# Building a routing table by adding single weights in DRAM in place of one-hot matmuls

## The chip, the cores and the metric

The kernel runs on one core of one Trainium2 chip. The metric is the device time of one execution in microseconds, the median of three runs.

## What is computed

The reference is two blocks, one behind the other, on 512 tokens of width 1024 in float32: first a two-layer block of modulated feed-forwards, a pooling mixer and a convolution mixer, then a block with stick-breaking attention, a recurrent branch and a retrieval layer over 16384 single-neuron experts. Only the retrieval layer (and the low parts of weights in it) is touched:

```python
q = jnp.einsum('td,dhk->thk', xc, w_query)                       # 8 heads, two halves of 128
s = jnp.einsum('thpk,hpnk->thpn', q, sub_keys)
top_s, top_i = lax.top_k(s, 16)                                  # 16 of 128 keys, per half
cand_s = top_s[:, :, 0, :, None] + top_s[:, :, 1, None, :]       # 256 pairs
best_s, best_pos = lax.top_k(cand_s, 16)
idx = take(cand_i, best_pos)                                     # cand_i = i0 * 128 + i1
g = jax.nn.softmax(best_s, axis=-1)
u, v = expert_u[idx], expert_v[idx]
act = jax.nn.gelu(jnp.einsum('td,thkd->thk', xc, u))
return jnp.einsum('thk,thkd->td', g * act, v)
```

So each token has 8 heads x 16 experts = 128 weights g, and a pair of heads may name the same expert, in which case their weights add.

## The kernel before

The kernel doesn't gather experts. It computes the activations of all 16384 experts for all 512 tokens, multiplies them by a dense table of weights (zero where a token hasn't chosen an expert), and multiplies the result by all of expert_v. Experts are numbered 128 n + m; a column m is the 128 experts with that m, n on the partitions, tokens along the free axis.

**The stream of weights.** All weight matrices come as 599 groups of 128 x 1024 float32 (512 KB) from DRAM. For each group c, SyncE loads `raw`, ScalarE rounds it to `whi` (line 499, helper `hi`), another engine forms the low part `wlo = raw - whi` (line 445, helper `lo`, on GpSimd throughout), and TensorE runs 24 matmuls of 512 columns (`three`, lines 1450 to 1452: high by high, high by low, low by high). There are four buffers of each, and `hi` of group c + 3 is issued beside group c.

**The up stage** is 128 groups, a column each: TensorE writes a bank, ScalarE applies the gelu (line 790) and stores 256 KB to the DRAM tensor `expert_acts` (line 783). **The down stage** is 128 groups too: for each column m a 256 KB piece of weights (`g_ring`, line 843) and of activations (`act_in`, line 844) is read back, VectorE multiplies them (`we32`, line 1426), ScalarE rounds, VectorE takes the rest (line 1430), and TensorE multiplies eight such columns at a time by eight groups of expert_v.

**The table.** In the up stage's first 32 columns (the lead: 8 columns for each 128 tokens) VectorE runs `best_pairs(tt)`: the top 16 of 256 pairs per head, the two expert numbers (`chosen[0]`, `chosen[1]`), the softmax (ScalarE's exponential, line 815, stands behind the eight columns in its queue). TensorE waits for `chosen_ready`, transposes the three rows (line 1765), and VectorE copies them to `pick` (`take_turned`), the weight split in three bf16 parts. In the columns 32 to 127, four sections of 16 columns with a chunk of 8 tokens each (64 chunks) and 8 without, `rows` on VectorE makes one-hot matrices (`hot_m`, `hot_n`, and `hot_w` by parts 0 and 1, lines 1405 to 1409), GpSimd the third part (line 465), and `sums` on TensorE multiplies them, 24 matmuls of 128 columns per chunk (line 1756). ScalarE copies the sums to `spread` (line 810), and after each section 8 MB go to the DRAM tensor `expert_weights` (lines 826 to 829). Before the last four columns ScalarE waits for the stores (`spilled`), then issues the first loads of the down stage.

Every engine runs its instructions in the order they are written; the order below is written out by hand in the code of each engine.

Of the kernel before, what the change touches and what calls it, by code (L numbers as in the profile page):

```python
# [93 lines left out]
BLK, MASK, MEAN_H, IDENT, IOTA = range(N_PLAIN)  # L94
# [10 lines left out]
TC = 8  # L105
# [3 lines left out]
CHUNKS = P // TC  # L109
GAP = 8  # L110
assert TT * (LEAD + CHUNKS + GAP) == NK and LEAD % 4 == GAP % 4 == CHUNKS % 4 == 0
LOWEST = -3.0e38
EARLY = NK // 2
# [18 lines left out]
def build(nc, stream, ada, smalls, consts, smalls2, consts2, keys, xin, out):  # L132
# [108 lines left out]
    chosen = place("chosen", 194, [P, 3, PH * TOP], F32)  # L241
    left = place("left", 195.5, [P, 2, P], F32)
    iota_b = place("iota_b", 202, [P, P], BF16)
    hot_n = place("hot_n", 177, [P, 2, TC, P], BF16)
    hot_m = place("hot_m", 181, [P, 2, TC, P], BF16)
    hot_w = place("hot_w", 185, [P, 2, 3, TC, P], BF16)
    pick = place("pick", 197, [P, 5, T], BF16)
    spread = place("spread", 100, [P, NK, P], F32)

    g_ring = place("g_ring", 172, [P, 4, T], F32)  # L250
    act_out = place("act_out", 164, [P, 4, T], F32)
    act_in = place("act_in", 185, [P, 4, T], F32)
    we32 = place("we32", 181, [P, 2, T], F32)
# [4 lines left out]
    expert_weights = nc.dram_tensor("expert_weights", (TT, P, NK, P), F32).ap()  # L258
# [101 lines left out]
    chosen_ready = sem("chosen_ready")  # L360
    turned = sem("turned")
    pick_step = sem("pick_step")
    iota_ready = sem("iota_ready")
    hot_mark = sem("hot_mark")
    hot_ready = sem("hot_ready")
    hot_third = sem("hot_third")
    hot_used = sem("hot_used")
    spread_ready = sem("spread_ready")
    spilled = sem("spilled")
    spilled_late = sem("spilled_late")  # L370
# [24 lines left out]

    def hot_column(part, c, i):

        cols = pick[:, part, TC * c:TC * c + TC] if i is None else pick[:, part, bass.ds(i * (4 * TC) + TC * c, TC)]
        return cols.unsqueeze(2).to_broadcast([P, TC, P])

# [10 lines left out]
    with nc.Block() as block:  # L411
# [29 lines left out]
        def _(pool):  # L441
# [15 lines left out]
            up = SEG["up"][0]  # L457
            lo_range(0, up + LOOK)

            def third_rows(c, i):  # L460

                pool.wait_ge(hot_mark, at(c + 1, i, 4))
                if c >= 2:
                    pool.wait_ge(hot_used, at(c - 1, i, 4))
                pool.tensor_tensor(hot_w[:, c % 2, 2, :, :], hot_m[:, c % 2, :, :], hot_column(4, c, i), ALU.mult).then_inc(hot_third, 1)  # L465

            def columns_run(m0, n):
                with pool.Fori(0, n // 4) as i:
                    for m in range(m0, m0 + 4):
                        lo(up + m + LOOK, i, 4)  # L470

            columns_run(0, TT * LEAD)
            for tt in range(TT):
                m0 = TT * LEAD + tt * (CHUNKS + GAP)
                c0 = tt * CHUNKS
                if tt == 0:
                    for k in range(4):
                        third_rows(c0 + k, None)
                        lo(up + m0 + k + LOOK, None, 0)
                    m0, c0 = m0 + 4, c0 + 4  # L480
                with pool.Fori(0, CHUNKS // 4 - (tt == 0)) as i:
                    for k in range(4):
                        third_rows(c0 + k, i)
                        lo(up + m0 + k + LOOK, i, 4)
                columns_run(TT * LEAD + tt * (CHUNKS + GAP) + CHUNKS, GAP)
            lo_range(up + NK + LOOK, n_groups)


        @block.scalar
        def _(act):  # L490
            def hi(c, i=None, m=0):

# [390 lines left out]
        def _(dve):  # L883
# [527 lines left out]
            for c in range(4):  # L1411
                rows(c, None)
# [471 lines left out]
```

## Time and profile before

| | |
|---|---|
| median of 3 runs | 3951.97 us (3945.84 to 3955.1) |
| span of the profiled execution, first to last instruction | 3949.3 us |
| busy PE / DVE / ACT / POOL | 3616.9 / 2232.4 / 1272.9 / 1693.6 us |
| mean granted TensorE clock | 0.957 of full speed |
| first to last gelu of the up stage | 2338.2 to 3238.2 us |
| first down product | 3243.6 us |

The profiled execution has no time of its own beside the runs' times; its span of 3949.3 us is 2.7 us below the median of the runs, which also holds what lies before the first and behind the last instruction. Below, a time within the execution is counted from the first instruction. A busy engine is one that executes, not one that is needed: the waits and the timeline say which of them the others wait for.

### The profile page before, as it was taken

What the parts mean: (1) busy time and instruction counts of PE and PEld (TensorE: products, weight loads), DVE (VectorE), ACT (ScalarE), POOL (GpSimd) and SP (SyncE); (2) the same over time, 40 slices, a digit from 0 to 9 for tenths busy, and PEclk for the clock granted to TensorE, in tenths of its full rate; (3) what the DMA queues carried; (4) which work ended last, traced back from release to release, by engine and by line L of the source; (5) the groups of instructions that cost most, each with busy time, mean ns of one, the idle gap of its engine ahead of it and who ended that gap; (6) DMA issues with size and microseconds to landing.
All of it is one profiled execution on the core that took longest, in us unless ns stands there. A gap on an engine that the chain in (4) does not pass through costs nothing.

```text
span 3949.3 us, 49496 instructions
## 1 busy us (share of the span) xinstructions
PE 3616.9 (92%) x16838; PEld 2965.4 (75%) x16838; DVE 2232.4 (57%) x2653; ACT 1272.9 (32%) x1600; POOL 1693.6 (43%) x667
## 2 busy tenths in 40 slices
PE   5999689998999899998887999889899889999999
PEld 4788568886888787886665787777777768888887
DVE  5662566506650543102757798795875946666663
ACT  2222332213221323222354323343343433333331
POOL 3444234443444343443220433465665644444443
PEclk9999889999999999999886999999999999999999
DMA  5554145424542222222110223325445376655563
GB/s 203 174 173 148 59 134 173 155 97 128 176 157 98 80 96 92 96 97 84 64 48 11 80 94 125 112 91 207 164 135 204 96 263 194 193 192 192 194 193 106
DMA packets 230845, 531.38 MB, mean 135 GB/s; under 512 B 20432, under 2 KB 86224, under 8 KB 228688
## 3 DMA queue, kind: packets, MB, share of 16 engines
q1 hardware_dynamic: 86976, 318.49, 24.7%
q10 hardware_dynamic: 143760, 211.43, 15.8%
q8 instruction: 69, 1.13, 0.1%
q14 instruction: 40, 0.33, 0.0%
HBM read 460.63 MB, written 69.21 MB: 134 GB/s over the span
## 4 chain that ended last, share of the span: by engine, by line
issue 38%; PE 34%; POOL 15%; DVE 11%; DMA 1%; ACT 1%; POOLq 0%; DVEq 0%; ACTq 0%
POOL wlo L445 15%; PE bank L1450 10%; PE bank L1452 10%; PE bank L1451 10%; DVE hot_w L1409 8%; PE bank L1756 1%; DVE hot_m L1405 1%; PE bank L1669 1%; DMA expert_acts<-act_out 0%; DVE rstd L936 0%; PE bank L1656 0%; PE bank L1644 0%; PE bank L1642 0%; PE bank L1643 0%; PE bank L1477 0%
## 5 line engine op out<-in xcount | busy, mean ns | idle before, releaser
L445 POOL TENSOR_TENSOR wlo<-raw,whi 128x1024 fp32r<-128x1024 f32 x599 | 1525.7, 2550 | 2112.3 <-ACT whi L499 2111.1
L1450 PE MATMUL bank<-hhi,whi 128*128 128x512 f32 x2832 | 1130.5, 399 | 33.1 <-DVE hlo L1065 22.9
L1451 PE MATMUL bank<-hlo,whi 128*128 128x512 f32 x2832 | 1117.6, 395 | 0.0
L1452 PE MATMUL bank<-hhi,wlo 128*128 128x512 f32 x2832 | 1116.4, 394 | 0.0
L499 ACT ACTIVATE whi<-raw 128x1024 fp32r<-128x1024 f32 x599 | 632.9, 1060 | 1210.7 <-PE bank L1452 1035.8
L1450 PEld LDWEIGHTS bank<-hhi,whi 128*128 128x128 f32 x2832 | 541.7, 191 | 148.0 <-issue 23.4
L1452 PEld LDWEIGHTS bank<-hhi,wlo 128*128 128x128 f32 x2832 | 541.1, 191 | 115.9
L1451 PEld LDWEIGHTS bank<-hlo,whi 128*128 128x128 f32 x2832 | 541.5, 191 | 112.4 <-issue 1.4
L894 DVE SCALAR_TENSOR_TENSOR ada_acc<-ada_raw,cond,ada_acc 128x512 f32<-128x512 f32 x224 | 371.8, 1660 | 80.7 <-DMA ada_raw<-ada_dram 72.0
L1450 PE MATMUL bank<-we,whi 128*128 128x512 f32 x1024 | 399.2, 390 | 13.4 <-DVE we L1430 13.4
L1451 PE MATMUL bank<-we,whi 128*128 128x512 f32 x1024 | 399.1, 390 | 0.0
L1452 PE MATMUL bank<-we,wlo 128*128 128x512 f32 x1024 | 398.9, 390 | 0.0
L1409 DVE TENSOR_TENSOR hot_w<-hot_m,pick 128x1024 bf16<-128x1024 bf16 x128 | 353.4, 2799 | 0.0
L1430 DVE TENSOR_TENSOR we<-we,we 128x512 fp32r<-128x512 f32 x128 | 261.7, 2044 | 95.5 <-ACT we L858 95.5
L1450 PE MATMUL bank<-uhi,whi 128*128 (+1 forms) x704 | 273.9, 389 | 0.0
L1451 PE MATMUL bank<-ulo,whi 128*128 (+1 forms) x704 | 273.9, 389 | 0.0
L1452 PE MATMUL bank<-uhi,wlo 128*128 (+1 forms) x704 | 273.9, 389 | 0.0
L963 DVE TENSOR_TENSOR u<-silu,bank 128x512 f32<-128x512 f32 x88 | 60.1, 683 | 308.4 <-PE bank L1452 287.2
L1450 PEld LDWEIGHTS bank<-we,whi 128*128 128x128 f32 x1024 | 192.7, 188 | 53.8 <-issue 13.8
L1451 PEld LDWEIGHTS bank<-we,whi 128*128 128x128 f32 x1024 | 192.7, 188 | 40.0
L1452 PEld LDWEIGHTS bank<-we,wlo 128*128 128x128 f32 x1024 | 192.7, 188 | 40.0
L465 POOL TENSOR_TENSOR hot_w<-hot_m,pick 128x1024 bf16<-128x1024 bf16 x64 | 168.4, 2632 | 117.7 <-DVE hot_m L1405 112.2
(232 smaller groups left out, 3398.1 us busy)
## 6 DMA issues: line engine op xcount, KB each, us to landing
raw<-stream_dram SPq DMA_DIRECT2D x599, 512.0 KB, 3.3
ada_raw<-ada_dram ACTq DMA_DIRECT2D x256, 256.0 KB, 3.9
expert_acts<-act_out ACTq DMA_DIRECT2D x128, 256.0 KB, 4.1
g_ring<-expert_weights ACTq DMA_DIRECT2D x128, 256.0 KB, 3.6
act_in<-expert_acts ACTq DMA_DIRECT2D x128, 256.0 KB, 3.7
first_raw<-ada_dram ACTq DMA_DIRECT2D x8, 1024.0 KB, 14.6
expert_weights<-spread ACTq DMA_DIRECT2D x2, 4096.0 KB, 17.9
x<-xin_dram SPq DMA_DIRECT2D x1, 2048.0 KB, 7.7
```

The lines of the kernel that those rows point to most:

```text
L445: pool.tensor_tensor(wlo[:, s, :, :], raw[:, s, :, :], whi[:, s, :, :].bitcast(F32), ALU.subtract).then_inc(lo_ready, 1)
L465: pool.tensor_tensor(hot_w[:, c % 2, 2, :, :], hot_m[:, c % 2, :, :], hot_column(4, c, i), ALU.mult).then_inc(hot_third, 1)
L499: act.activation(whi[:, s, :, :], raw[:, s, :, :], ACT.Copy).then_inc(hi_ready, 1)
L894: dve.scalar_tensor_tensor(acc[:, :], ada_raw[:, u % 4, :], cond[:, k:k + 1], acc[:, :], ALU.mult, ALU.add).then_inc(ada_used, 1)
L963: dve.tensor_tensor(u32[:, j % 2, :], silu[:, j % 2, :], psum[2 * (j % 2) + 1][:, :], ALU.mult).then_inc(u_mul, 1)
L1405: dve.tensor_tensor(hot_m[:, s, :, :], numbers, hot_column(1, c, i), ALU.is_equal).then_inc(hot_mark, 1)
L1409: dve.tensor_tensor(hot_w[:, s, part, :, :], hot_m[:, s, :, :], hot_column(2 + part, c, i), ALU.mult).then_inc(hot_ready, 1)
L1430: dve.tensor_tensor(we[:, b % 2, 1, j, :], we32[:, m % 2, :], we[:, b % 2, 0, j, :].bitcast(F32), ALU.subtract).then_inc(we_ready, 1)
L1450: pe.matmul(bank, whi[:, s, b, :], rhi, start=start, stop=False)
L1451: pe.matmul(bank, whi[:, s, b, :], rlo, start=False, stop=False)
L1452: return pe.matmul(bank, wlo[:, s, b, :], rhi, start=False, stop=stop)
L1669: pe.matmul(out, sq_round[:, TRI if j == i else ONES, :], part[:, h % 2, ATT_OFF[j]:ATT_OFF[j] + n], start=False, stop=False, skip_group_c ...
```

## The change

The dense table is no longer built on the core. `expert_weights` becomes a DRAM tensor of shape (column m, n, token). It is first filled with zeros from a new input of zeros, by 22 DRAM to DRAM transfers on ScalarE's queue, one for each tile of the fourth feed-forward (`zero_fill`, six columns or 1.5 MB each, four in the last two). Then, for each 128 tokens, VectorE computes for each of the 128 choices a cell number, `128 * 512 * i1 + 512 * i0 + token`, and the weight; GpSimd issues 128 indirect transfers, each of which adds 128 single float32 weights (one for each token, so one for each partition) to their cells. After the 16 of a head it waits until they have landed, since two heads of a token can name the same cell. The transposes, `pick`, the one-hot matrices, the sums and `spread` go. ScalarE waits for all 512 transfers (`scattered`) where it waited for the stores. The low parts of the up and down groups, from the fourth up group on, are formed by VectorE in place of GpSimd; in the selection they stand between its steps.

The core of the diff:

```diff
+            pool.wait_ge(zeroed, 16 * FT)
             for tt in range(TT):
...
+                pool.wait_ge(gain_ready, tt + 1)
+                for h in range(PH):
+                    for r in range(TOP):
+                        e = h * TOP + r
+                        pool.indirect_dma_start(weight_cells, bass.IndirectOffsetOnAxis(ap=cell[:, tt, e:e + 1], axis=0),
+                                                pay[:, tt, e:e + 1], None, compute_op=ALU.add).then_inc(scattered, 16)
+                    pool.wait_ge(scattered, 16 * TOP * (PH * tt + h + 1))
...
+            def zero_fill(j, i):
+
+                m0 = ZERO_M * j
+                n = ZERO_M if j < BODY * BODIES else (NK - ZERO_M * BODY * BODIES) // 2
...
+                act.dma_start(dst.rearrange("m n t -> n m t"), zeros[0:n].rearrange("m n t -> n m t")).then_inc(zeroed, 16)
...
+            columns_run(TT * LEAD, NK - TT * LEAD - 4)
...
-            act.wait_ge(spilled, 16 * TT)
+            act.wait_ge(scattered, 16 * TT * PH * TOP)
...
+            def lo(c, i=None, m=0):
+                s = c % R
+                dve.wait_ge(hi_ready, at(c + 1, i, m))
+                dve.tensor_tensor(wlo[:, s, :, :], raw[:, s, :, :], whi[:, s, :, :].bitcast(F32), ALU.subtract).then_inc(lo_ready, 1)
...
+                lo(ahead + 7)
+                sel(dve.tensor_scalar(row_t[:, :], chosen[:, 0, :], float(T), sq_plain[:, TOKEN, tt:tt + 1], ALU.mult, ALU.add))
+                seld()
+                sel(dve.scalar_tensor_tensor(cell[:, tt, :], chosen[:, 1, :], float(NK * T), row_t[:, :], ALU.mult, ALU.add))
+                seld()
+                dve.tensor_tensor(pay[:, tt, :].rearrange("p (h r) -> p h r", h=PH), expo[:, :, :],
+                                  esum[:, 1, :].unsqueeze(2).to_broadcast([P, PH, TOP]), ALU.mult).then_inc(gain_ready, 1)
...
+            with dve.Fori(0, (last - first) // R) as i:
+                for c in range(first, first + R):
+                    lo(c, i, R)
...
+                    if b and v_group(b - 1, j) + LOOK < n_groups:
+                        lo(v_group(b - 1, j) + LOOK, i, 2 * MB)
...
+            columns_run(0, NK)
```

GpSimd's queue behind the last of its low parts, first before (the loop over four mixed columns) and then changed (the whole rest of its program). L465 is the third bf16 part of a one-hot product, L445 and L426 are a group's low part, L446 is the indirect transfer:

```order
L465 TENSOR_TENSOR hot_w<-hot_m,pick 128x1024
L444 REGISTER_ALU
L445 TENSOR_TENSOR wlo<-raw,whi 128x1024
L462 REGISTER_ALU
L464 REGISTER_ALU
L465 ISA
L465 TENSOR_TENSOR hot_w<-hot_m,pick 128x1024
L444 REGISTER_ALU
L445 TENSOR_TENSOR wlo<-raw,whi 128x1024
```

```order
L426 TENSOR_TENSOR wlo<-raw,whi 128x1024 x2
L446 DMA expert_weights<-pay,cell 8388608x1 x512
L392 UNCONDITIONAL_BRANCH
```

What remains on GpSimd in the up and down stages is 512 transfers without anything between them but waits.

VectorE's queue at the end of the selection for one 128 tokens, before:

```order
L1366 TENSOR_REDUCE chosen<-prod 128x128
L1369 TENSOR_REDUCE esum<-expo 128x8
L1371 RECIPROCAL esum<-esum 128x8
L1373 TENSOR_TENSOR chosen<-expo,esum 128x128
L1388 CAST pick<-bank 128x2x128
L1389 CAST pick<-bank 128x128
L1390 TENSOR_TENSOR left<-bank,pick 128x128
L1391 CAST pick<-left 128x128
L1392 TENSOR_TENSOR left<-left,pick 128x128
L1393 CAST pick<-left 128x128
L1331 TENSOR_TENSOR cand<-top_v 128x2048
```

and changed, where the same reduction is L1326, a low part L1280 and the next selection's first step L1287:

```order
L1280 TENSOR_TENSOR wlo<-raw,whi 128x1024
L1326 TENSOR_REDUCE chosen<-prod 128x128
L1329 TENSOR_REDUCE esum<-expo 128x8
L1331 RECIPROCAL esum<-esum 128x8
L1280 TENSOR_TENSOR wlo<-raw,whi 128x1024
L1334 TENSOR_SCALAR row_t<-chosen,sq_plain 128x128
L1336 SCALAR_TENSOR_TENSOR cell<-chosen,row_t 128x128
L1338 TENSOR_TENSOR pay<-expo,esum 128x128
L1280 TENSOR_TENSOR wlo<-raw,whi 128x1024
L1287 TENSOR_TENSOR cand<-top_v 128x2048
```

The six small steps on `pick` are gone, two small steps and eight low parts of 128 x 1024 per 128 tokens have come in, and the next selection no longer stands behind a product of TensorE.

## Rows read from the trace of the kernel before

**Rows 1.** The page: span, busy time of each engine, clock (tenths, 40 slices).

```profile
span 3949.3 us, 49496 instructions
...
PE 3616.9 (92%) x16838; PEld 2965.4 (75%) x16838; DVE 2232.4 (57%) x2653; ACT 1272.9 (32%) x1600; POOL 1693.6 (43%) x667
```

**Rows 2.** Four windows: us; busy PE, PEld, DVE, ACT, POOL; clock; DMA share; GB/s.

```profile
2337.00:2531.00 194.00, 180.65 (x780) 148.61 (x779) 147.45 (x365) 74.69 (x85) 77.36 (x31) 0.96 0.38 126
2531.00:3192.00 661.00, 589.65 (x3668) 485.22 (x3667) 523.92 (x259) 271.70 (x311) 406.52 (x153) 0.98 0.42 145
3192.00:3243.00 51.00, 38.21 (x169) 31.32 (x167) 15.71 (x16) 15.98 (x23) 18.43 (x8) 0.91 1.02 371
3243.00:3945.00 702.00, 698.28 (x3072) 577.96 (x3072) 413.14 (x369) 208.85 (x245) 309.50 (x125) 1.00 0.56 180
```

**Rows 3.** Waits in the mixed columns: who waited for whom, total, times, longest.

```profile
DVE hot_m L1405 <- PE bank L1756: 129.6, 3, 43.2
...
PE bank L1756 <- DVE hot_w L1409: 71.3, 44, 5.1
```

**Rows 4.** Timeline of VectorE, one chunk of the mixed columns: start, length.

```profile
2819.09 3.41 DVE L1409 TENSOR_TENSOR hot_w<-hot_m,pick 128x1024 bf16<-128x1024 bf16 x1
2822.43 1.21 DVE L1405 TENSOR_TENSOR hot_m<-iota_b,pick 128x1024 bf16<-128x1024 bf16 x1
...
2824.70 6.25 DVE L1409 TENSOR_TENSOR hot_w<-hot_m,pick 128x1024 bf16<-128x1024 bf16 x2
```

**Rows 5.** Timeline of ScalarE in the lead: eighth column, exponential.

```profile
2343.66 0.60 ACT L790 ACTIVATE act_out<-bank 128x512 f32<-128x512 f32 x1 [3.89 <-PE bank L1452]
...
2376.30 0.60 ACT L790 ACTIVATE act_out<-bank 128x512 f32<-128x512 f32 x1 [3.89 <-PE bank L1452]
...
2378.21 0.31 ACT L815 ACTIVATE expo<-below 128x128 f32<-128x128 f32 x1
```

**Rows 6.** Timeline of VectorE, selection for the first 128 tokens.

```profile
2342.89 2.29 DVE L1331 TENSOR_TENSOR cand<-top_v 128x2048 f32<-128x2048 f32 x1
...
2366.90 1.22 DVE L1361 TENSOR_TENSOR prod<-is_pos,top_b 128x2048 bf16<-128x2048 bf16 x1
...
2372.81 3.30 DVE L1361 TENSOR_TENSOR prod<-is_pos,top_b 128x2048 bf16<-128x2048 bf16 x1
...
2379.18 0.29 DVE L1373 TENSOR_TENSOR chosen<-expo,esum 128x128 f32<-128x128 f32 x1
```

**Rows 7.** Timeline of ScalarE at the hand-over to the down stage.

```profile
3203.05 0.60 ACT L790 ACTIVATE act_out<-bank 128x512 f32<-128x512 f32 x1 [3.89 <-PE bank L1452]
...
3215.22 0.60 ACT L790 ACTIVATE act_out<-bank 128x512 f32<-128x512 f32 x1 [10.62 <-DMA expert_acts<-act_out]
...
3215.91 0.41 ACTq L843 DMA_DIRECT2D g_ring<-expert_weights  x1
...
3238.15 0.58 ACT L790 ACTIVATE act_out<-bank 128x512 f32<-128x512 f32 x1
```

**Rows 8.** Instructions of the tile we: first down product, VectorE's share.

```profile
L1450 PE MATMUL bank<-we,whi x1024: 387/389/767, 3243.6 to 3941.1; 128*128 128x512 f32 x171
...
L1430 DVE TENSOR_TENSOR we<-we,we x128: 692/2111/2403, 3224.6 to 3895.0; 128x512 fp32r<-128x512 f32 x128
```

**Rows 9.** DMA issues of the page: KB each, us from issue to landing.

```profile
expert_acts<-act_out ACTq DMA_DIRECT2D x128, 256.0 KB, 4.1
...
small<-smalls_dram ACTq DMA_DIRECT2D x1, 33.5 KB, 1.8
```

**Rows 10.** Window in the fourth feed-forward, columns as in rows 2.

```profile
1514.00:1742.00 228.00, 228.00 (x1008) 188.85 (x1007) 31.13 (x48) 67.12 (x86) 101.02 (x44) 1.00 0.30 99
```

**Rows 11.** DMA of 0.9 us with many small packets.

```profile
DMA packets 157, 0.07 MB, mean 75 GB/s; under 512 B 144, under 2 KB 144, under 8 KB 157
...
q10 hardware_dynamic: 157, 0.07, 49.9%
```

**Rows 12.** Groups of GpSimd in the lead.

```profile
L445 POOL TENSOR_TENSOR wlo<-raw,whi 128x1024 fp32r<-128x1024 f32 x31 | 77.4, 2495 | 113.2 <-ACT whi L499 113.2
```

More of the change, by code:

```diff
@@ L129, in v_group, with build @@
     return SEG["down"][0] + MB * b + d
-def build(nc, stream, ada, smalls, consts, smalls2, consts2, keys, xin, out):
+def build(nc, stream, ada, smalls, consts, smalls2, consts2, keys, zeros, xin, out):
     KB = 1024
@@ L454, in lo_range @@
                     lo(c, None, 0)
[L457 to L472, printed above, removed]
-            for tt in range(TT):
[L474 to L486, printed above, removed]
+            lo_range(0, SEG["up"][0] + LOOK)
+            pool.wait_ge(zeroed, 16 * FT)
+            for tt in range(TT):
+                pool.wait_ge(gain_ready, tt + 1)
[5 more added lines that the diff above has]
+                    pool.wait_ge(scattered, 16 * TOP * (PH * tt + h + 1))
         @block.scalar
@@ L866, in _ @@
                 load_column(m, None)
-            for k in range(GAP // 2):
-                column(NK - GAP // 2 + k, None)
+            for k in range(4):
+                column(NK - 4 + k, None)
                 out_step(0, None, range(2 * k, 2 * k + 2))
             store_acts(NK - 1, None)
-            act.wait_ge(spilled_late, 16)
             for k in range(4):
@@ L1363, in best_pairs @@
                     seld()
-                    if half == 0 and tt:
-                        dve.wait_ge(turned, tt)
+                    lo(ahead + 5 + half)
                     sel(dve.tensor_reduce(chosen[:, half, :].rearrange("p (h r) -> p h r", h=PH), prod[:, :, :, :], AXX, ALU.add))
@@ L1395, in _ @@
+            dve.wait_ge(lo_ready, up + LOOK)
             for tt in range(TT):
                 best_pairs(tt)
-                take_turned(tt)
-            def rows(c, i):
-                s = c % 2
-                if c >= 2:
-                    dve.wait_ge(hot_used, at(c - 1, i, 4))
-                    dve.wait_ge(hot_third, at(c - 1, i, 4))
-                numbers = iota_b[:, :].unsqueeze(1).to_broadcast([P, TC, P])
-                dve.tensor_tensor(hot_m[:, s, :, :], numbers, hot_column(1, c, i), ALU.is_equal).then_inc(hot_mark, 1)
-                dve.tensor_tensor(hot_n[:, s, :, :], numbers, hot_column(0, c, i), ALU.is_equal).then_inc(hot_ready, 1)
-                dve.wait_ge(hot_mark, at(c + 1, i, 4))
-                for part in range(2):
-                    dve.tensor_tensor(hot_w[:, s, part, :, :], hot_m[:, s, :, :], hot_column(2 + part, c, i), ALU.mult).then_inc(hot_ready, 1)
@@ L1411, in _, with out_step @@
-            for c in range(4):
-                rows(c, None)
-            with dve.Fori(0, T // TC // 4 - 1) as i:
-                for c in range(4, 8):
-                    rows(c, i)
-            def out_step(b, i):
-                for j in range(MB):
+            first = up + LOOK + TT * LEAD
+            last = up + NK + LOOK - 4
+            with dve.Fori(0, (last - first) // R) as i:
+                for c in range(first, first + R):
+                    lo(c, i, R)
+            def out_step(b, i, js=range(MB)):
+                for j in js:
@@ L1436, in out_step @@
                         dve.tensor_tensor(x[:, j, :], psum[j][:, :], x[:, j, :], ALU.add).then_inc(y_added, 1)
-            out_step(0, None)
+            for k in range(4):
+                lo(last + k)
+                out_step(0, None, range(2 * k, 2 * k + 2))
             out_step(1, None)
```

141 lines of the change are left out of this document (32 added, 109 removed).

## The prediction, made blind

> **What bounds the kernel now.** I read the page first. TensorE is busy 92% of a span of 3949.3 us [rows 1]; VectorE with 57% and GpSimd with 43% look harmless, but these are means over unlike stages. The windows say more [rows 2]. In the down stage TensorE is busy 698.28 of 702 us, and nothing that shortens another engine's work can help there. The up stage is unlike that: it runs from about 2332.8 (the second gelu starts at 2343.66, two columns later, [rows 5]) to the first down product at 3243.6 [rows 8], 911 us for 128 columns. A column costs TensorE 5.44 us when nothing hinders it: from the gelu at 2343.66 to that at 2376.30 there are six columns, 32.64 us [rows 5]. 128 of them are 696 us. So some 215 us of the up stage are not needed for its groups, and this is all that the change can bring.
>
> Where are they? In the mixed columns VectorE is busy 523.92 of 661 us [rows 2], and the waits name TensorE's product of one-hot matrices waiting for hot_w [rows 3]. The timeline gives the rhythm: one chunk's hot_m starts at 2822.43 and its second hot_w ends at 2824.70 + 6.25 = 2830.95: 8.5 us, against 5.44 for a column [rows 4]. 64 chunks by 3.0 us are 192 us. The rest is in the lead (PE busy 180.65 of 194) and in the hand-over (38.21 of 51) [rows 2].
>
> **The change part by part.** *The one-hot work goes*: the columns 32 to 127 then cost TensorE 96 x 5.44 = 522 us, if low parts arrive in time.
>
> *Low parts on VectorE.* A subtraction of 128 x 1024 float32 isn't there on VectorE. The cand step of 128 x 2048 takes 2.29 us, half of it 1.15 [rows 6]; the subtraction of 128 x 512 takes 0.69 when GpSimd is idle, twice it 1.38 [rows 8]. I take 1.2. In the mixed columns and the down stage that is 1.2 of 5.44 us and hidden: VectorE's down work is about 0.7 + 0.7 + 0.7 + 1.2 = 3.3 of 5.44, and GpSimd's 2.5 us [rows 12] that it replaces was longer. A low part is issued three groups ahead, so a delay under some 10 us reaches nobody.
>
> *The lead* has no such slack. The first selection runs from 2342.89 to 2379.18 + 0.29, 36.6 us [rows 6]; one of its prod steps took 3.30 us and the other 1.22, and such stretching beside GpSimd's subtraction goes away, so 34.5. Add eight low parts (9.6) and three small steps (0.9): 45 us per 128 tokens, against 8 x 5.44 = 43.5 for TensorE. VectorE becomes the bound of the lead by a little: 4 x 45 = 180 us. TensorE no longer waits for the transposes. The exponential still stands behind the eighth gelu (2376.30, then 2378.21, [rows 5]); VectorE arrives there later than it does now, so nothing is added. Lead end: 2332.8 + 180 = 2512.8. Up end: 2512.8 + 522.2 = 3035.0. From the last gelu to the first down product the trace has 3243.6 - 3238.15 = 5.4 us [rows 7, 8]. So without any wait for the table the first down product is at 3040.4, 203.2 us earlier.
>
> *The filling with zeros* adds 33.5 MB over the 22 tiles of the fourth feed-forward, 240 us: 140 GB/s to the 99 GB/s there, at a DMA share of 0.30 [rows 10]; the hand-over shows that 371 GB/s can flow [rows 2]. Counted once it is hidden; counted twice (read and write) 379 would be asked of 371, at most 5 us. I take 0. GpSimd's wait for it was over 600 us earlier and costs nothing.
>
> *The 512 adding transfers* decide. They start when the first selection is done, 2342.9 + 45 = 2388, and the later three selections come every 45 us, faster than 128 transfers go. Let one cost g on average, waits included; they end at E = 2388 + 512 g. ScalarE stands at its wait for them with the last four columns and all of the down stage behind it. TensorE has rounded weights for three more columns, then stops too. What follows E is what followed the stores before: first load of g_ring issued at 3215.91, first down product at 3243.6, 27.7 us [rows 7, 8]. So the first down product is at the later of 3040.4 and E + 27.7. The table costs nothing while 2388 + 512 g + 27.7 < 3040.4, g < 1.22 us; the gain is used up at E = 3215.9, g = 1.62 us; between, the time against the median 3952 (the span is 2.7 less) is 3952 - 3215.9 + 2388 + 512 g = 3124 + 512 g.
>
> What is g? No transfer issued by GpSimd is in the trace. From below: ScalarE issues a DMA in 0.41 us [rows 7], and the fastest small one lands in 1.8 us [rows 9]: 0.41 + 1.8 / 16 = 0.52. From above: GpSimd's subtraction, 2.50 us [rows 12], with the store's landing of 4.1 us [rows 9] per 16: 2.76; and, if each went alone, 4.1. To choose, I count the addresses that GpSimd must work out: 2.50 / 1024 = 2.4 ns for an element per partition; two descriptors for each of 128 weights are 256 x 2.4 ns = 0.62, three (the old value too) 0.94; with the issue 1.03 or 1.35. I take 1.1, plus 4.1 / 16 = 0.26 for the wait behind each head: g = 1.36, E = 3084, time 3124 + 696 = **3820 us**. The DMA engines: small packets took 0.499 x 16 x 0.9 / 157 = 46 ns of an engine [rows 11]; with 8 weights per engine and one to three packets for each that is 0.37 to 1.1 us in the 0.58 of the time that the stage's loads leave free [rows 2], so 0.6 to 1.9: mostly under the issue, but no proof.
>
> *A shared port.* VectorE's hot_w takes 3.41 us beside GpSimd, its hot_m of the same shape a fraction [rows 4], and line 1430 has 692 ns at least and 2111 in the median [rows 8]: the two engines hold each other up. If that also stops GpSimd while it makes transfers, it loses VectorE's 1.2 of each 5.44 us: 1.1 / 0.78 = 1.41, g 1.67, time 3979. The Trainium skill (SBUF — State Buffer, section on the two separate sides) states such a rule: the pair is an exclusive lock, taken by a VectorE instruction with two SBUF inputs against one of GpSimd that reads SBUF, and a locked-out GpSimd cannot write descriptors. By that rule the change would just lose (rival 4). The trace agrees as to compute instructions; no row shows it for transfers.
>
> **The rivals.**
> 1. *The table is hidden* (g under 1.22): 3952 - 203 = 3749 us. For it: the issue of 0.41 us. Against: 128 addresses each and a landing of 1.8 to 4.1 us per head. 0.27.
> 2. *My forecast*, g 1.22 to 1.60: 3749 to 3943. 0.36.
> 3. *Slower, since one transfer costs more than 1.62 us* of GpSimd's time: place, GpSimd's queue in the up stage, with ScalarE waiting before column 124; price 512 us for each us. By the third descriptor with the longest landing it would be 1.61, by the DMA engines' packets up to 1.9, so for g 1.64 to 2.0: 3964 to 4148. 0.12.
> 4. *The shared port* stretches each issue by VectorE's share: g 1.67, 3979. For it: the stretched rows of both engines; against: a transfer has little to read. 0.08.
> 5. *The transfers go one at a time*, each with its round trip of 2.0 (only the 33.5 KB load lands faster) to 4.1 us [rows 9]: 4148 to 5223. Against: nothing in the program waits between the 16 of a head. 0.14. The Trainium skill (DMA: Bandwidth & Descriptors, section on the anatomy of one DMA on the gpsimd path) fits 2.0 us of fixed cost to each transfer, mostly the receipt from memory; by it, an estimate, 512 in turn are 1024 us and the time 4148. No row here shows a transfer of that path.
> 6. *It cancels out*, g 1.60 to 1.64: 0.03.
>
> **How the numbers follow.** A measurement of this kernel tells 0.2% (8 us) from no change. Faster: 0.27 + 0.36 = 0.63; same 0.03; slower 0.12 + 0.08 + 0.14 = 0.34. The likeliest is the second case, 3820. Its own range is 3749 to 3943. The low end is the hidden table less 6 us for a lead that TensorE alone bounds (4 x 1.5), and a few for what I rounded: 3740. The high end is where the round trip decides, g = 2.0: 4150. That leaves out case 5 and little else.
>
> **What would show it.** The mixed columns at 5.44 us from gelu to gelu; VectorE's low part at 1.2 us; a lead of 180 us; first transfer near 2388; TensorE idle only between column 126 and the last, with ScalarE waiting for the 512th landing near 3084; 27.7 us from there to the first down product. The prediction is wrong if GpSimd's issue is far from 1.1 us, if the wait behind a head is far from 4 us, if the low parts or the selection are stretched beside the transfers so that columns take over 5.44 us, or if the adding packets delay the stream of weights, which would show as ScalarE waiting for raw.

## The result and the profile after

The changed kernel takes 4177.98 us (median of 4 runs, 4171.02 to 4181.82), beside 3952.76 us (3945.84 to 3955.1) for the kernel before on the same chip: 1.0578 times as long, 95% interval 1.056 to 1.0597. The change makes the kernel 225 us slower. The profiled execution has a span of 4180.0 us.

The windows of the changed kernel, in the columns of [rows 2], stand for the lead, the other columns, the stretch in which everything waits for the table, the hand-over, and the down stage:

```profile
2337.00:2531.00 194.00, 194.00 (x858) 160.61 (x857) 172.80 (x404) 80.91 (x92) 114.83 (x64) 1.00 0.56 141
2531.00:3040.00 509.00, 495.79 (x2188) 410.19 (x2186) 108.00 (x88) 200.56 (x221) 393.28 (x242) 0.99 0.60 138
3040.00:3440.00 400.00, 0.00 (x0) 0.00 (x0) 0.00 (x0) 0.00 (x0) 314.72 (x205) 0.50 0.22 0
3440.00:3480.00 40.00, 14.88 (x42) 11.57 (x43) 17.08 (x22) 12.55 (x18) 5.29 (x4) 0.60 0.73 244
3480.00:4175.00 695.00, 692.62 (x3056) 573.18 (x3054) 395.16 (x491) 206.94 (x244) 0.00 (x0) 1.00 0.55 180
```

Up to 3027 TensorE is saturated, in the lead too (495.79 us of the second window are 2531 to 3027); then for over 400 us the only engine that works is GpSimd, with 206 of its 512 instructions still to go at 3040. The down stage is what it was. ScalarE's timeline shows where the program stands:

```profile
3010.51 0.60 ACT L763 ACTIVATE act_out<-bank 128x512 f32<-128x512 f32 x1 [3.64 <-PE bank L1389]
...
3447.78 0.35 ACTq L792 DMA_DIRECT2D g_ring<-expert_weights  x1
...
3450.65 1.06 ACT L461 ACTIVATE whi<-raw 128x1024 fp32r<-128x1024 f32 x1 [439.54 <-issue]
```

The gelu of column 123 is at 3010.51; the next rounding of weights, 440 us later, stands behind the wait for the transfers, and so does the first load of the down stage at 3447.78 (in [rows 7] it was at 3215.91). In the instructions of the tile we, the first down product is then at 3473.4, against 3243.6 in [rows 8]; these 229.8 us are the whole loss (the spans differ by 230.7):

```profile
L1387 PE MATMUL bank<-we,whi x1024: 387/389/764, 3473.4 to 4171.8; 128*128 128x512 f32 x171
```

What the transfers cost is in two rows of the groups (busy and mean ns, then the idle time ahead of them by what ended it) and one of the DMA queues:

```profile
L446 POOL DMA_INDIRECT expert_weights<-pay,cell x512 | 828.1, 1617 | 288.0 <-issue 168.4 <-DMA expert_weights<-pay,cell 62.6 <-DVE pay L1338 57.0
L1280 DVE TENSOR_TENSOR wlo<-raw,whi 128x1024 fp32r<-128x1024 f32 x253 | 310.0, 1225 | 872.3 <-ACT whi L461 871.7
...
q0 software_dynamic: 73728, 0.29, 5.0%
```

In g, the average cost of a transfer in the forecast's sum, there are then three parts: 828.1 / 512 = 1.617 us of instruction, 168.4 / 512 = 0.33 us between instructions, and 62.6 / 512 = 0.12 us of waits for a head's landing. The sum is 2.07 us, and 2387.1 + 512 x 2.07 = 3447, the first load. GpSimd's timeline, behind a head and within the next, shows the same in single instructions:

```profile
3291.46 1.54 POOL L446 DMA_INDIRECT expert_weights<-pay,cell  x1 [1.63 <-DMA expert_weights<-pay,cell]
3293.30 1.54 POOL L446 DMA_INDIRECT expert_weights<-pay,cell  x1 [0.30 <-issue]
3295.15 1.54 POOL L446 DMA_INDIRECT expert_weights<-pay,cell  x1 [0.30 <-issue]
```

Within a head there is a transfer every 1.84 us, with no other engine at work, no semaphore waited for, and a share of 0.22 for the DMA engines (third window). So the time is spent on GpSimd, and the DMA engines have room; what GpSimd does within an instruction the trace doesn't show. Ten of the gaps within heads are longer, 1.8 to 5.1 us each and 25 us together; four of them come every 113 transfers, in the run with writing transfers below too. What they are stays open.

### The profile page after: what moved, and what is told of

Same layout as the page of the kernel before. It is cut to its first block, busy times and chain, and to the rows that moved or that the text cites. A ratio compares the mean times of both kernels' runs of the same rounds, so it can differ in the third digit from the quotient of the medians.

```text
span 4180.0 us, 45233 instructions
## 1 busy us (share of the span) xinstructions
PE 3508.9 (84%) x15278; PEld 2879.9 (69%) x15278; DVE 1826.0 (44%) x2634; ACT 1205.0 (29%) x1510; POOL 1706.2 (41%) x862
## 3 DMA queue, kind: packets, MB, share of 16 engines
q0 software_dynamic: 73728, 0.29, 5.0%
## 4 chain that ended last, share of the span: by engine, by line
issue 39%; POOL 32%; PE 24%; DMA 3%; DVE 2%; ACT 1%; POOLq 0%; ACTq 0%; DVEq 0%
POOL expert_weights L446 19%; POOL wlo L426 14%; PE bank L1387 7%; PE bank L1389 7%; PE bank L1388 7%; DMA expert_weights<-pay,cell 3%; PE bank L1606 1%; DVE rstd L883 0%; PE bank L1593 0%; PE bank L1581 0%; PE bank L1579 0%; PE bank L1580 0%; PE bank L1414 0%; PE bank L1409 0%; PE bank L1654 0%
## 5 line engine op out<-in xcount | busy, mean ns | idle before, releaser
L426 POOL TENSOR_TENSOR wlo<-raw,whi 128x1024 fp32r<-128x1024 f32 x346 | 877.9, 2541 | 1451.7 <-ACT whi L461 1450.5
L446 POOL DMA_INDIRECT expert_weights<-pay,cell x512 | 828.1, 1617 | 288.0 <-issue 168.4
L1280 DVE TENSOR_TENSOR wlo<-raw,whi 128x1024 fp32r<-128x1024 f32 x253 | 310.0, 1225 | 872.3 <-ACT whi L461 871.7
L1387 PEld LDWEIGHTS bank<-we,whi 128*128 128x128 f32 x1024 | 192.9, 188 | 52.6 <-issue 12.5
L527 ACT ACTIVATE uhi<-u 128x512 f32 (+1 forms) x88 | 55.6, 632 | 426.7 <-DVE u L910 426.7
```

The source lines that it names most:

```text
L426: pool.tensor_tensor(wlo[:, s, :, :], raw[:, s, :, :], whi[:, s, :, :].bitcast(F32), ALU.subtract).then_inc(lo_ready, 1)
L446: pool.indirect_dma_start(weight_cells, bass.IndirectOffsetOnAxis(ap=cell[:, tt, e:e + 1], axis=0), pay[:, tt, e:e + 1], None, compute_op= ...
L527: act.activation(uhi[:, j, :] if i is None else uhi[:, bass.ds(i * BODY + j, 1), :].rearrange("p a t -> p (a t)"), u32[:, j % 2, :], ACT.C ...
L1280: dve.tensor_tensor(wlo[:, s, :, :], raw[:, s, :, :], whi[:, s, :, :].bitcast(F32), ALU.subtract).then_inc(lo_ready, 1)
L1387: pe.matmul(bank, whi[:, s, b, :], rhi, start=start, stop=False)
```

## The experiments

The theory after the result: each adding transfer costs GpSimd about 1.54 us of instruction and 0.30 us to the next one; all else went as forecast. The rivals: the transfers wait for one another (landings of about 2 us); VectorE's use of a shared port stretches them; the low parts on VectorE or the filling with zeros cost something in other places.

### Half of the transfers: is all else as forecast?

```diff
-                    for r in range(TOP):
+                    for r in range(TOP // 2):
...
-                    pool.wait_ge(scattered, 16 * TOP * (PH * tt + h + 1))
+                    pool.wait_ge(scattered, 16 * (TOP // 2) * (PH * tt + h + 1))
```

> Only 8 of the 16 transfers of each head are issued, so half of the weights are missing from the table; all else as changed. Theory (the 512 transfers on GpSimd alone set the end, everything else of the change is as fast as forecast): the last lands near 2387 + 256 x 1.95 + 32 x 2.0 = 2950, before TensorE is done with the up groups, so the first down product comes at about 3035 to 3045 and the time is 3735 to 3755 us, about 5% under the kernel before. Rival (low parts on VectorE, the filling with zeros or the loads beside the transfers also cost time, hidden so far behind the transfers): 3770 us or more, with columns over 5.45 us apart. Rival 2 (the cost is in the landing, not in the number): half the transfers save less than half, over 3900 us.

It took 3742.92 us (3733.09 to 3746.8), 0.948 of before (0.9464 to 0.9497). Below are its transfers, its first down product, and a window in the columns:

```profile
L446 POOL DMA_INDIRECT expert_weights<-pay,cell x256: 1538/1541/2575, 2388.4 to 2953.3; - x128
```

```profile
L1387 PE MATMUL bank<-we,whi x1024: 389/389/763, 3038.9 to 3736.8; 128*128 128x512 f32 x171
```

```profile
2531.00:2960.00 429.00, 429.00 (x1894) 355.24 (x1893) 96.43 (x79) 180.05 (x198) 313.01 (x196) 1.00 0.63 145
```

The last transfer is issued at 2953, before ScalarE asks for it, and TensorE doesn't stop: 429.00 of 429 us beside 196 transfers. The first down product is at 3038.9 (forecast for a hidden table: 3040.4) and the time 3743 (forecast: 3749). This kernel leaves out half of the weights, so it is a measurement and no gain. It says that the change would win 3243.6 - 3038.9 = 204.7 us if the transfers cost no wait, and that the changed kernel waits 3473.4 - 3038.9 = 434.5 us for them.

### What one transfer costs: 64 weights, and writing in place of adding

```diff
-                        pool.indirect_dma_start(weight_cells, bass.IndirectOffsetOnAxis(ap=cell[:, tt, e:e + 1], axis=0),
-                                                pay[:, tt, e:e + 1], None, compute_op=ALU.add).then_inc(scattered, 16)
+                        pool.indirect_dma_start(weight_cells, bass.IndirectOffsetOnAxis(ap=cell[0:64, tt, e:e + 1], axis=0),
+                                                pay[0:64, tt, e:e + 1], None, compute_op=ALU.add).then_inc(scattered, 16)
```

> Each of the 512 transfers adds 64 weights in place of 128 (the tokens in the upper 64 partitions of each block of 128 are missing from the table). Theory A (GpSimd works out address by address, cost proportional to the weights): one instruction falls from 1.54 to about 0.8 us, and the time to about 3124 + 512 x (0.8 + 0.3 + 0.12 + 0.1) = 3800 us. Theory B (a fixed cost of each instruction): it stays at 1.5 us or more and the time at 4150 to 4180. My own count at the prediction, 0.41 fixed and 2.4 ns for each of two or three descriptors, would give 1.0 to 1.1.

One run: 4101.25 us. The transfers (their median instruction is the middle of the first three numbers, in ns) and their queue:

```profile
L446 POOL DMA_INDIRECT expert_weights<-pay,cell x512: 1400/1407/2677, 2387.4 to 3364.8; - x171
...
L446 POOL DMA_INDIRECT expert_weights<-pay,cell x512 | 763.9, 1492 | 271.8 <-issue 153.2 <-DMA expert_weights<-pay,cell 61.6 <-DVE pay L1338 57.0
...
q0 software_dynamic: 40960, 0.16, 3.1%
```

Half the weights save 0.134 us of the median of 1.541: 2.1 ns a weight. By that slope, an estimate from two sizes, 128 weights are 0.27 us of the instruction, and the rest, 1.27 us and the 0.30 us behind it, is paid for each transfer.

```diff
-                                                pay[:, tt, e:e + 1], None, compute_op=ALU.add).then_inc(scattered, 16)
+                                                pay[:, tt, e:e + 1], None).then_inc(scattered, 16)
```

> The 512 transfers write the weight in place of adding it (where two heads of a token name the same expert the table holds one weight in place of the sum). Theory (GpSimd's instruction sets the pace, and adding costs it no descriptor more): 1.54 us each as before and 4170 to 4180 us; the wait behind a head shorter by some tenths, at most 20 us in all. Rival (the adding, a third descriptor or the reading of the old value, is what makes it slow): one instruction at about 1.1 to 1.2 us and the time near 3950 to 4000.

One run: 3871.61 us, 75 us under the kernel before (3947.05), with a table that is wrong where two heads meet. The instruction, the groups and the queue:

```profile
L446 POOL DMA_INDIRECT expert_weights<-pay,cell x512: 953/959/2945, 2386.2 to 3136.1; - x171
...
L446 POOL DMA_INDIRECT expert_weights<-pay,cell x512 | 538.7, 1052 | 269.2 <-issue 158.2 <-DVE pay L1338 57.0 <-DMA expert_weights<-pay,cell 54.1
...
q0 software_dynamic: 16384, 0.29, 0.3%
```

I had expected no difference, and was wrong: the adding itself costs GpSimd 0.58 us in each (1.541 to 0.959), 298 of the 306 us by which the run is faster. The queue says what is different: a writing transfer is 16384 / 512 = 32 packets, an adding one 73728 / 512 = 144, and with 64 weights 40960 / 512 = 80. That is a packet for each weight and 16 more where it adds; the 32 where it writes would be two for each of the 16 DMA engines, which the view doesn't tell apart. At the 2.1 ns above, the 112 packets more are 0.23 us of the 0.58; the rest of the price of adding stays open. For the DMA engines the packets are cheap: 5.0% of 16 x 4180 us over 73728 is 45 ns of an engine (the 46 ns of [rows 11]), 0.41 us of the 1.84 us that a transfer has.

The saving can be had where nothing is there to add to, in the first head of each 128 tokens:

```diff
-                                                pay[:, tt, e:e + 1], None, compute_op=ALU.add).then_inc(scattered, 16)
+                                                pay[:, tt, e:e + 1], None, **({"compute_op": ALU.add} if h else {})).then_inc(scattered, 16)
```

> The changed kernel, but the 16 transfers of the first head of each block of tokens, which meet only zeros, write in place of adding (64 of 512); the table is the same. Theory (adding costs GpSimd 0.58 us more per instruction than writing, 1.54 against 0.96, whatever stands around it): 64 x 0.58 = 37 us less, about 4141 us. Rival (the difference comes from rows of adding transfers that back up one another): less than 15 us.

It took 4147.47 us (4137.48 to 4147.75), 1.0494 of before (1.0475 to 1.0512): 30.5 us less than the changed kernel for 64 transfers, 0.48 each, where 37 were forecast and each kernel's runs lie some 10 us apart. In the traces GpSimd's busy time falls by 33.6 us (828.1 to 794.5), 0.53 each. So the saving is there in a full computation too, over the rival's 15 us.

### Are they one behind the other? Heads of three blocks in turns

Each block of 128 tokens counts its landings on its own semaphore, and GpSimd issues a head of the second, third and fourth block in turn, so that two other heads lie between a head and the wait for it.

```diff
+            for tt, h in [(0, h) for h in range(PH)] + [(tt, h) for h in range(PH) for tt in range(1, TT)]:
+                if h == 0:
+                    pool.wait_ge(gain_ready, tt + 1)
+                else:
+                    pool.wait_ge(scattered_by[tt], 16 * TOP * h)
```

> The same 512 transfers in another order: the heads of the first 128 tokens as now, then head by head in turn for the three other blocks of tokens, each with its own semaphore, so that before a head's transfers the landing waited for is 32 transfers old. Theory (the waits behind the heads are 62.6 us of GpSimd's time, 2.0 us each): 23 of 31 waits vanish, 45 us less, about 4130 us. Rival (the wait only gathers time that the DMA engines need for the adds anyway, and the stall moves into the issue): no change, over 4170 us, with instructions longer than 1.54 us.

It took 4133.55 us (4126.55 to 4135.62), 1.0473 of before (1.0456 to 1.049). GpSimd's waits in it:

```profile
POOL expert_weights L448 <- issue: 161.8, 504, 5.0
POOL expert_weights L448 <- DMA expert_weights<-pay,cell: 15.5, 7, 3.3
```

Of 62.6 us of waiting for landings 47.1 went, and the time fell by 44.4. The wait is 62.6 / 31 = 2.0 us behind a head, paid once for its sixteen, and other heads in between hide it. The list of DMA issues of this run has the landing of single transfers, where the changed kernel's had none:

```profile
expert_weights<-pay,cell POOLq DMA_INDIRECT x512, 3.0
```

From the start of GpSimd's instruction to the landing are 3.0 us in the median, and the next transfer starts after 1.84: one is still under way when GpSimd begins the next.

### The parts that were costed at nothing

In the kernel before, the low parts of the down stage alone go to VectorE (GpSimd's `lo_range` over them goes, VectorE's `out_step` gets the `lo` of the change):

```diff
+                    if b and v_group(b - 1, j) + LOOK < n_groups:
+                        lo(v_group(b - 1, j) + LOOK, i, 2 * MB)
```

> The kernel before with one part of the change alone: in the down stage VectorE forms the low parts in place of GpSimd (125 groups); one-hot matmuls and all else as before. Theory (the down stage is TensorE's, low parts are three groups ahead): no difference, within 0.2% of the kernel before, groups 5.44 us apart, and VectorE's line 1430 falls from 2.11 to 0.69 us since GpSimd no longer works beside it. Rival (a second low-part worker in VectorE's queue, behind its wait for TensorE, comes too late): down groups over 5.5 us apart and at least 10 us more.

3950.45 us beside 3949.25: a ratio of 1.0004 (0.9995 to 1.0013). Its rest of the products on VectorE, where [rows 8] had a median of 2111 ns, and its low part:

```profile
L1436 DVE TENSOR_TENSOR we<-we,we x128: 692/693/2105, 3222.3 to 3894.3; 128x512 fp32r<-128x512 f32 x128
```

```profile
L1419 DVE TENSOR_TENSOR wlo<-raw,whi x125: 1225/1226/1226, 3245.7 to 3919.0; 128x1024 fp32r<-128x1024 f32 x125
```

Without GpSimd's subtraction beside it VectorE's runs three times as fast, and nothing comes of it: from the first to the last down product are 697.4 us, as before (697.5).

In the changed kernel, a second DRAM tensor is filled with zeros beside the first:

```diff
+                dst = spare[m0:m0 + n] if i is None else spare[bass.ds(i * (ZERO_M * BODY) + m0, n)]
+                act.dma_start(dst.rearrange("m n t -> n m t"), zeros[0:n].rearrange("m n t -> n m t")).then_inc(zeroed, 16)
```

> The changed kernel with the filling with zeros doubled: each of the 22 tiles also fills as much of a spare DRAM tensor. The first gelu of the up stage came at 2341.4 in the changed kernel and at 2338.2 before. Theory (the filling is hidden behind the loads of the stream, the 3 us are scatter between executions): TensorE stays busy 228 of 228 us in the window 1514 to 1742 or nearly, the first gelu at 2337 to 2345, the time 4170 to 4190. Rival (DMA bandwidth: 99 GB/s + 2 x 140 is about the 371 seen as a maximum): TensorE waits for weights in this window, the first gelu at 2350 to 2450 and the time as much longer.

One run: 4178.26 us, the same. The fourth feed-forward, to be read beside [rows 10], once with one filling (the changed kernel) and once with two:

```profile
1514.00:1742.00 228.00, 228.00 (x1007) 188.80 (x1006) 32.63 (x52) 70.61 (x87) 103.00 (x43) 1.00 0.70 242
```

```profile
1514.00:1742.00 228.00, 227.81 (x1006) 188.28 (x1005) 46.70 (x53) 66.50 (x84) 97.95 (x41) 1.00 1.02 365
```

The DMA share goes from 0.30 to 0.70 to 1.02, and TensorE's stream of weights isn't disturbed (228.00 and 227.81 of 228 us busy). From 99 to 242 GB/s is 143 x 228 us = 33 MB: the filling counts once in this column, as I had reckoned in the forecast's first case (239).

### A version between the two kernels

If 256 transfers are hidden, the table can be shared: tokens 0 to 255 by transfers, 256 to 511 by one-hot sums. 32 chunks are put in two sections of 32 columns with a chunk for every two columns, all three bf16 parts are made by VectorE, since GpSimd is busy, and ScalarE copies the sums to `spread` and stores them behind each section.

```diff
+    MIXED = ((TT * LEAD, 0), (TT * LEAD + 48, CHUNKS))
...
+            def mixed(m0, c0, i):
+                for k in range(2):
+                    lo(up + m0 + 2 * k + LOOK, i, 4)
+                    marks(c0 + k, i)
+                    lo(up + m0 + 2 * k + 1 + LOOK, i, 4)
+                    parts(c0 + k, i)
```

> Half and half, whole computation: the first two blocks of 128 tokens by 256 adding transfers, the other two by one-hot matmuls (32 chunks in 64 of the 96 mixed columns, one chunk per two columns, all five one-hot steps on VectorE, GpSimd left to its transfers). Theory (transfers cost 2.07 us each and are hidden if they end by 3012; one-hot work costs only what TensorE spends on it if VectorE has room): transfers end near 2388 + 530 = 2918; VectorE needs 2.4 + 2 x 1.2 x 2 + 6 = about 8.5 to 9.5 of 10.9 us per two columns; TensorE pays 1.6 to 2.0 us for each of 32 chunks and 3 to 5 us for each of two transposes: 3743 + 32 x 1.8 + 8 = 3809, range 3795 to 3830, 3.5% under the kernel before. Rival (VectorE's one-hot steps are stretched beside GpSimd's transfers as they were beside its subtractions, 1.2 to 2.9 us): VectorE bounds the mixed columns at 14 us or more per two, 3850 or more.

3874.38 us (3870.45 to 3879.09), 0.9809 of before (0.9795 to 0.9823): 1.9% faster than the kernel before, but 65 us over the 3809 expected. Two places in the trace held the rest. VectorE's timeline over two columns and a chunk:

```profile
2567.83 1.23 DVE L1334 TENSOR_TENSOR wlo<-raw,whi 128x1024 fp32r<-128x1024 f32 x1 [4.68 <-ACT whi L486]
2568.97 1.22 DVE L1433 TENSOR_TENSOR hot_m<-iota_b,pick 128x1024 bf16<-128x1024 bf16 x1
2570.11 1.22 DVE L1434 TENSOR_TENSOR hot_n<-iota_b,pick 128x1024 bf16<-128x1024 bf16 x1
2572.11 1.22 DVE L1334 TENSOR_TENSOR wlo<-raw,whi 128x1024 fp32r<-128x1024 f32 x1 [0.78 <-ACT whi L486]
2573.25 3.49 DVE L1440 TENSOR_TENSOR hot_w<-hot_m,pick 128x1024 bf16<-128x1024 bf16 x3
2581.42 1.23 DVE L1334 TENSOR_TENSOR wlo<-raw,whi 128x1024 fp32r<-128x1024 f32 x1 [4.68 <-issue]
```

VectorE works 8.4 of 13.6 us, yet the sums wait for hot_w, 13 times and 15.3 us in all in the window behind the lead, which is what TensorE is short of there:

```profile
2531.00:2710.00 179.00, 163.71 (x945) 134.25 (x944) 106.77 (x92) 66.62 (x79) 142.70 (x80) 1.00 0.52 115
```

The hot_w steps stand behind low parts that wait for ScalarE's rounding, and ScalarE comes to that only behind the copy of the last chunk's sums and a gelu. And ScalarE's timeline behind the first section:

```profile
2745.01 0.41 ACTq L833 DMA_DIRECT2D expert_weights<-spread  x1
...
2748.49 26.87 ACTq L781 DMA_DIRECT2D expert_acts<-act_out  x1
2775.46 1.06 ACT L486 ACTIVATE whi<-raw 128x1024 fp32r<-128x1024 f32 x1 [26.60 <-issue]
```

A store of 8 MB in pieces of 512 bytes (128 tokens of a row of 512) is ahead in ScalarE's queue, and the next store takes 26.87 us to issue instead of 0.34. Each place has its run. First, the one-hot matrices one chunk ahead:

```diff
+            marks(0, None)
+            parts(0, None)
...
-                    marks(c0 + k, i)
+                    if k < n:
+                        marks(c0 + k + 1, i)
...
-                    parts(c0 + k, i)
+                    if k < n:
+                        parts(c0 + k + 1, i)
```

> The kernel that shares the table between the two ways (tokens 0 to 255 by 256 transfers, 256 to 511 by one-hot sums) took 3874.4, 65 more than I had worked out. Theory: about 40 of these are an order of VectorE's queue. The one-hot parts of a chunk stand behind the low part of a group whose high part ScalarE makes only behind the gelu of the column just finished, so TensorE's sums wait 1.2 for them at every chunk, and two columns with a chunk take 13.5 where 10.9 + 1.3 are work. Here the one-hot matrices of a chunk are made one chunk earlier, all else as it was: two columns and a chunk in about 12.3, the whole in 3874 - 32 x 1.2 = about 3836 (3825 to 3845). Rival: TensorE's sums wait for ScalarE's copies of the sums (the banks), not for VectorE, and then nothing changes (3870 to 3880).

3829.96 us (3828.79 to 3841.56), 0.971 of before (0.9692 to 0.9729). The same rhythm, from a low part to the next but one, is now 12.5 us (2560.45 to 2572.96), and in the same window TensorE has no gap any more:

```profile
2560.45 1.22 DVE L1334 TENSOR_TENSOR wlo<-raw,whi 128x1024 fp32r<-128x1024 f32 x1 [0.80 <-ACT whi L486]
...
2572.96 1.23 DVE L1334 TENSOR_TENSOR wlo<-raw,whi 128x1024 fp32r<-128x1024 f32 x1 [0.97 <-ACT whi L486]
```

```profile
2531.00:2710.00 179.00, 179.00 (x1038) 148.59 (x1037) 118.84 (x103) 73.54 (x87) 144.65 (x80) 1.00 0.56 128
2710.00:2800.00 90.00, 76.76 (x347) 63.03 (x346) 19.00 (x16) 22.99 (x28) 68.25 (x43) 0.92 0.85 209
```

The second line still has the stall behind the store. The next run adds to this edit a DRAM tensor of its own for the one-hot half, laid out as in the kernel before, 64 KB in a piece for each partition:

```diff
+    spread_weights = nc.dram_tensor("spread_weights", (TT - ADDED, P, NK, P), F32).ap()
...
+                act.dma_start(spread_weights[b], spread[:, :, :]).then_inc(spilled, 16)
...
+                act.dma_start(g_ring[:, s, 0:HALF_T], g).then_inc(g_landed[s], 16)
+                act.dma_start(g_ring[:, s, HALF_T:T].rearrange("p (a t) -> p a t", a=TT - ADDED), w).then_inc(g_landed[s], 16)
```

> The edit of the run before, and the one-hot half of the table in a DRAM tensor of its own, laid out as in the kernel before (one piece of 64 KB for each partition), in place of pieces of 512 bytes in the common table; the down stage then loads a column's weights with two transfers of 128 KB, not one of 256 KB. Theory: the store of 8 MB in small pieces fills ScalarE's DMA queue; in the shared kernel the next store of activations took 26.9 to be issued behind it, and TensorE stood still for 17 of 90 us; at the second store again, 17 of 107. Both go: 3836 - 30 = about 3805 (3790 to 3815). Rival: the store waits for bandwidth, not for its number of pieces, and the stall stays (3830 to 3840). Either way half of the saving can come back in the down stage, if the 128 further loads delay it; its span, 695 in the changed kernel, shows that.

3803.24 us (3799.83 to 3805.05), 0.963 of before (0.9615 to 0.9645). The window behind the first store, and the first issue behind it on ScalarE's queue:

```profile
2710.00:2800.00 90.00, 90.00 (x416) 74.60 (x415) 24.29 (x20) 28.60 (x35) 59.59 (x38) 1.00 0.80 236
```

```profile
2717.29 0.35 ACTq L834 DMA_DIRECT2D spread_weights<-spread  x1
...
2721.00 0.34 ACTq L782 DMA_DIRECT2D expert_acts<-act_out  x1
```

More bytes flow in the same window (236 to 209 GB/s), at a lower share, and TensorE isn't held up: the bytes of the store were not the trouble. Its pieces of 512 bytes are the likely one; the edit also gives this half of the table a DRAM tensor of its own, and no run tells the two apart. This version does the whole computation, 145 us under the kernel before and 375 under the changed one. Its first down product is at 3093.2, 54 us behind that of the run with half of the transfers.

## Why the prediction was wrong, by its own steps

**The failing step** is the price of the transfer, "I take 1.1, plus 4.1 / 16 = 0.26". By the trace it is 1.617 + 0.33 = 1.95 us of GpSimd's time and 0.12 us of waiting. The first is 0.85 us more, times 512 is 433 us; the second 0.14 less, 70 us; 3820 + 433 - 70 = 4183, against a measured 4178. So the path and the formula 3124 + 512 g were right (with 2.07 it gives 4184), and its one unknown was mis-sized. How it went wrong can be read off the experiments. I built the price from descriptors by 2.4 ns each (0.62 or 0.94 us) on a base of 0.41 us, ScalarE's issue in [rows 7]. The measured slope is 2.1 ns for a weight, 0.27 us for 128, where I had two or three descriptors of 2.4 ns. The base is 1.27 us, three times ScalarE's, of which the adding accounts for up to 0.58; and I had no term for the 0.30 us between two such instructions, though with 512 in a row this is 168 us. The lower bound, 0.52, and the upper, 2.76, did hold the truth; what failed is the choice between them, and a range that ended at g = 2.0, 0.07 short: above it I had left room only for transfers that go one at a time.

**The rivals.** The mechanism that happened is the third one: GpSimd's own time for each transfer, over the 1.62 us at which the gain is used up. I gave it 0.12 and a span of g from 1.64 to 2.0, and even that was too low. The fifth, each transfer with its round trip, gives by its lower end nearly the time that was measured (4148), and is yet refuted: transfers are issued 1.84 us apart with no wait between them and land 3.0 us after their start, and with the heads in turns 47 us of waits vanish. That its number comes so near is chance. The Trainium skill (DMA: Bandwidth & Descriptors, the anatomy of one DMA on the gpsimd path) fits 2.0 us of fixed cost to a transfer. The runs have a cost of that size, 3.0 us from the start of GpSimd's instruction, of which 1.54 are the instruction, and 2.0 of waiting behind a head; they show that such a cost is waited for once in sixteen transfers, so it doesn't set their pace.

**The shared port** exists for transfers, and is small. In the changed kernel an instruction takes 1.79 us in the lead (114.83 / 64), 1.63 in the columns and 1.54 with VectorE at rest; all stretches together are 828.1 - 512 x 1.541 = 39 us. Where they fall is seen in the timelines, in the lead and then in the columns, GpSimd's rows ahead of VectorE's:

```profile
2416.34 1.54 POOL L446 DMA_INDIRECT expert_weights<-pay,cell  x1 [0.30 <-issue]
2418.19 2.37 POOL L446 DMA_INDIRECT expert_weights<-pay,cell  x1 [0.30 <-issue]
...
2708.54 1.54 POOL L446 DMA_INDIRECT expert_weights<-pay,cell  x1 [0.30 <-issue]
```

```profile
2414.54 2.28 DVE L1326 TENSOR_REDUCE chosen<-prod 128x128 f32<-128x2048 bf16 x1
...
2416.85 2.29 DVE L1319 TENSOR_TENSOR is_pos<-iota_b,pos_b 128x2048 bf16<-128x2048 bf16 x1
...
2709.29 1.23 DVE L1280 TENSOR_TENSOR wlo<-raw,whi 128x1024 fp32r<-128x1024 f32 x1 [5.81 <-ACT whi L461]
```

The transfer that starts at 2418.19, 0.95 us before is_pos with its two inputs ends, takes 0.83 us longer. The one that starts within the reduction, which has one input, takes its 1.54, and so does the one at 2708.54, whose middle a low part falls into. Over all 512 it is the same: the 39 us lie in 79 transfers that start while VectorE is in a low part, an is_pos or a cand, each with two inputs (three that start together with one are not held), and the 86 others during which such an instruction begins take 1.54 to 1.55 us. So a transfer is held if VectorE is in such an instruction as it starts, until about its end, and not later on. That is read from the trace of one execution, and no run tests it by itself. The Trainium skill (SBUF — State Buffer, section on the two separate sides) has this lock as an exclusive one, which a VectorE instruction with two SBUF inputs takes against a GpSimd instruction that reads SBUF, and the trace agrees as to which instructions hold up a transfer. I had priced it as if it stopped all of a transfer, 0.31 us on each; the trace has 39 / 512 = 0.08. VectorE isn't held up in turn: its low part takes 1200 to 1297 ns, and in the version that shares the table hot_w takes 3.49 us for three.

**The other steps.** Low part on VectorE: 1.2 forecast, 1.225 measured. The one-hot work gone: columns at 5.44 us, from 2341.4 to 3010.5 for 123 of them. The lead was forecast VectorE-bound at 180 us, and was not: TensorE is busy 194.00 of 194, so it took 174. VectorE's share of it was mis-sized by a little: its last step on `pay` comes first at 2385.9 and the fourth time at 2514.8, 43.0 us for a selection with its low parts, not 45. The up stage began 3 us later in this execution, and the two cancel in part (first down product without a wait 3038.9 to 3040.4). First transfer: 2388 forecast, 2387.1. Filling: 0 forecast, 0 measured, and 0 for twice as much. From the first load to the first down product: 27.7 forecast, 25.6 measured. The table hidden: 3749 forecast, 3743 measured with half of the transfers. The granted clock was not in the forecast: it is 0.50 in the 400 us without a product, TensorE's lower level of 1.2 GHz, and 0.60 in the 40 us behind it. No cost of it is seen: these 25.6 us are under the 27.7 of before, and the last down product starts 698.4 us behind the first, against 697.5.

## What to carry to other kernels

An indirect transfer of 128 single weights costs GpSimd 1.0 us (writing) to 1.5 us (adding), and 0.3 us to the next; with half of the weights an adding one costs 1.4 (other sizes were not run). So count transfers, not bytes or weights, and find how many fit under the work beside them (here some 300 of 512, by (3040 - 27 - 2388) / 2.07, an estimate) before moving all of the work to them. Where an offloaded queue ends last, share the work out between the old way and the new: here half and half beats each, by 145 and 375 us. And on an engine that serves two chains in order, put the work that others wait for one step ahead of the work that itself waits.

## What was not expected of the hardware

- An adding indirect transfer occupies GpSimd for 1.54 us, a writing one for 0.96, and 0.30 us lie between two of them, with no other engine at work.
- An adding transfer of 128 single float32 weights is 144 packets, a writing one 32; yet 144 packets of 45 ns on 16 engines are no bound: the DMA share is 0.22 while nothing but the transfers runs.
- A VectorE instruction with two inputs holds up a transfer that starts while it runs, and not one that has started before: 39 us over 512 transfers.
- Behind a store of 8 MB in pieces of 512 bytes the next issue on the same queue takes 26.87 us; behind one with pieces of 64 KB, in a tensor of its own, it takes 0.34.
- A DMA share of 1.02 at 365 GB/s beside TensorE's stream of weights didn't slow it: 227.81 of 228 us busy.
